# The routing chain between the output projection and the first expert pair: logits turned earlier, one square moved, first gathers by token tile

## What is computed

```
logits = (t @ w_router + b_router)            # 32 experts, t = rmsnorm(x)
top_v, top_i = lax.top_k(logits, TOP_K)       # 4 of 32
wts = softmax(top_v)
z = xb @ w_up[e] + b_up[e]                    # per expert, on its tokens
y = x_glu * sigmoid(1.702 * x_glu) * (x_lin + 1)
out += wts * (y @ w_down[e] + b_down[e])      # then residual and final rmsnorm
```

## Time and profile before

| what | value |
|---|---|
| runs | 1147.6, 1148.07 (median), 1148.33 us |
| span of the profiled execution, first to last instruction | 1146.0 us |
| PE busy | 1113.5 us (97%) |
| DVE, ACT, POOL busy | 311.8, 229.6, 34.0 us |
| HBM read | 436.00 MB |
| mean rate over the span | 383 GB/s |

### The profile page before, as it was taken

One profiled execution on the slowest core, in us unless ns is written; L12 is line 12 of the kernel. 1 busy time (PEld: TensorE's weight loads), 2 busy tenths in 40 slices (PEclk: granted clock), 3 DMA queues, 4 the chain that ended last, 5 costly groups with the idle time before them and its releaser, 6 DMA issues.

```text
span 1146.0 us, 14903 instructions
## 1 busy us (share of the span) xinstructions
PE 1113.5 (97%) x5772; PEld 493.6 (43%) x5772; DVE 311.8 (27%) x785; ACT 229.6 (20%) x642; POOL 34.0 (3%) x69
## 2 busy tenths in 40 slices
PE   8999999999999999999999999999999999999997
PEld 6687778844333424333333333323232323232432
DVE  5665544032131221212130312121213030312123
ACT  4564363422020202010101111111111101010103
POOL 0200012210000000000000000000000000000000
PEclk9999999999999999999999999999999999999999
DMA  9743636989999999999999999999999999999995
GB/s 350 265 153 111 187 112 265 426 350 421 427 428 426 426 427 428 428 428 428 427 428 428 430 429 428 427 428 429 429 429 427 427 428 429 429 427 427 426 427 238
DMA packets 40802, 437.90 MB, mean 382 GB/s; under 512 B 6720, under 2 KB 9040, under 8 KB 11072
## 3 DMA queue, kind: packets, MB, share of 16 engines
q1 hardware_dynamic: 40136, 435.65, 91.2%
q10 hardware_dynamic: 624, 1.68, 0.4%
HBM read 436.00 MB, written 2.41 MB: 383 GB/s over the span
## 4 chain that ended last, share of the span: by engine, by line
PE 69%; DMA 24%; DVE 3%; ACT 2%; issue 1%; DVEq 0%; SPq 0%; ACTq 0%
PE bank L1319 21%; DMA ring<-in_w_down 20%; PE bank L1355 19%; PE bank L1055 8%; PE bank L1100 5%; PE bank L1201 4%; DMA area<-in_w_down 3%; PE bank L1222 3%; PE bank L1150 2%; PE bank L1235 1%; PE bank L1198 1%; PE bank L1036 1%; PE bank L1225 1%; DVE area L1748 1%; PE bank L923 1%
## 5 line engine op out<-in xcount | busy, mean ns | idle before, releaser
L1319 PE MATMUL bank<-ring,area 128*64 128x512 f32 x1744 | 396.4, 597 | 9.1 <-DMA ring<-in_w_up 8.7
L1319 PEld LDWEIGHTS bank<-ring,area 128*64 128x64 f32 x1744 | 117.2, 136 | 261.8 <-issue 222.9
L1355 PE MATMUL bank<-ring,area 128*64 128x512 f32 x928 | 213.7, 599 | 7.5 <-DMA ring<-in_w_down 7.5
L1736 DVE TENSOR_TENSOR x_tok<-x_tok,bank 128x512 f32<-128x512 f32 x60 | 41.3, 688 | 328.0 <-PE bank L1222 328.0
L800 ACT ACTIVATE area<-area 128x256 f32<-128x256 f32 x64 | 26.7, 417 | 516.3 <-DVE area L1748 516.3
L1055 PE MATMUL bank<-ring 128*128 128x264 f32 (+1 forms) x512 | 121.7, 393 | 0.0
L1355 PEld LDWEIGHTS bank<-ring,area 128*64 128x64 f32 x928 | 62.4, 136 | 117.9 <-issue 102.7
L1055 PEld LDWEIGHTS bank<-ring 128*128 128x128 f32 x512 | 95.2, 190 | 21.3 <-issue 4.0
L1773 DVE TENSOR_TENSOR area<-area 128x1024 f32<-128x1024 f32 x15 | 18.4, 1225 | 211.3 <-ACT area L810 211.3
L1222 PE MATMUL bank<-area 128*128 128x512 f32 x128 | 71.8, 644 | 0.0
L1319 PE MATMUL bank<-area 128*64 128x512 f32 x304 | 69.2, 597 | 1.5 <-DMA area<-in_w_up 1.5
(11 more groups left out here) (271 smaller groups left out, 702.6 us busy)
## 6 DMA issues: line engine op xcount, KB each, us to landing
ring<-in_w_up SPq DMA_DIRECT2D x103, 2048.0 KB, 34.3
ring<-in_w_down SPq DMA_DIRECT2D x51, 2048.0 KB, 33.9
area<-in_w_up SPq DMA_DIRECT2D x17, 2048.0 KB, 29.8
ring<-in_w_in SPq DMA_DIRECT2D x16, 1024.0 KB, 9.3
ring<-in_w_down SPq DMA_DIRECT2D x13, 1024.0 KB, 10.6
ring<-in_w_up SPq DMA_DIRECT2D x12, 1024.0 KB, 9.7
area<-in_w_down SPq DMA_DIRECT2D x5, 2048.0 KB, 34.3
ring<-in_w_out SPq DMA_DIRECT2D x8, 1024.0 KB, 5.0
```

What stands on the lines that cost most here:

```text
L1319: m = mm(bank[2 * h + n][64 * e:64 * e + 64, :], xe[:, k, 64 * e:64 * e + 64], w[:, kk, e, NB * n:NB * (n + 1)], start=False, stop=(k == K ...
L1355: m = mm(bank[4 + c][64 * e:64 * e + 64, :], y_t[:, 4 * half + f, 64 * e:64 * e + 64], w[:, f, e, :], start=False, stop=(half == 1 and f = ...
L1736: eng.tensor_tensor(x, x, combined_bank(unit, last)[:, :], ALU.add).then_inc(s.added, 1)
```

## The change

The logits of blocks 0 to 6 are turned by DVE and PE around the eighth block: DVE copies them to `lt` (now in `rs` and `rs_tail`) before it waits for that block, PE multiplies tiles 0 and 1 by `stack` where two dummy matmuls stood, and tile 2 after the transposes. Block 7's logits are computed token-major (`last_logits`) straight into the same PSUM rows. The block's second token tile is turned into bank 4, where DVE copies and squares it; ACT makes the two other squares, copies only tile 0, and takes the first bf16 part from `x_tok`. `rank_m` is made for the first two experts, then the one-hots in three instructions by token tile, then `rank_m` for the other 30. PE has three dummy matmuls instead of four ahead of the gather and waits for `rp_step`, `flag_ready` and `split_copy`; it then goes by token tile, in each tile the slot row, block 0 and block 1 (21 matmuls in all, as before). The dummy matmuls before the biases are four instead of six.

```diff
--- before.py
+++ after.py
@@ -179,7 +179,7 @@
 pt_done pt_evac_a pt_evac_v pv_done pv_evac qd_ready dsc_done dsc_ready dst_done
 q2_ready d_p_ready last_p_tr q2_p_ready d_pv_done d_pv_ready q2_pv_done q2_pv_ready sinkcol_step
 x_biased x_negmax x_sink_exp x_exp x_scaled attn_gated wout_used final_added x2_ready
-split_copy split_sub h2_tr logits_done negtop top_exp selb_ready rank_done flag_ready tables_ready gather_oh weight_oh
+split_copy split_sub h2_tr logits_done negtop top_exp selb_ready rank_done flag_ready tables_ready oh_tile own_rows first_rows rank_ready gather_oh weight_oh
 gather_done xt_ready up_done glu_ready lin_ready sig_ready gated_ready y_ready ytr_done yt_ready gwt_tr
 gwt_ready yd_ready combine_done added ring_used window_stored 
 y_final stored router_step lru_step x_step
@@ -296,10 +296,8 @@
         gw_t, o = at(o, [1, 2 * P + 64])
         assert o == MOE
         y_e, yd, gw_t, rrow = y_e[:, 0, :], yd[:, 0, :], gw_t[:, 0, :], rrow[:, 0, :]
-        lt, o = at(SLOT, [1, 2 * P + 96])
-        lt = lt[:, 0, :]
-        lt_trio = lt[:, 2 * P:2 * P + 96].rearrange("p (i c) -> p i c", i=3)[:, :, 0:B_S]
-        assert o <= 2 * KB * T
+        lt = rs[:, :, :].rearrange("p a b -> p (a b)")
+        lt_trio = rs_tail[:, 0:96].rearrange("p (i c) -> p i c", i=3)[:, :, 0:B_S]
         stack = h0[:, 0:E_N // B_S, :].rearrange("p a b -> p (a b)")
         LG = E_N + TOP_K
         lg, o = at(sig_at, [3, LG])
@@ -756,19 +754,27 @@
             for m in range(KB):
                 tb, cols, half = bank[2 + m % 2], slice(P * m, P * (m + 1)), m // (KB // 2)
                 eng.wait_ge(s.h2_tr, m + 1)
-                for t in range(3):
+                for t in range(3) if m < KB - 1 else (0, 2):
                     n = P if t < 2 else TRIO
                     act(parts[0:n, t % 2, 2 - t // 2, cols], tb[0:n, P * t:P * (t + 1)], ACT.Square, accum_out=ss[0:n, t, m:m + 1])\
                         .then_inc(s.squares, 1)
                 both = tb[:, 0:2 * P].rearrange("p (t c) -> p t c", t=2)
-                act(x_tok[:, :, cols], both, ACT.Copy)
+                if m < KB - 1:
+                    act(x_tok[:, :, cols], both, ACT.Copy)
+                else:
+                    act(x_tok[:, 0, cols], tb[:, 0:P], ACT.Copy).then_inc(s.first_rows, 1)
                 if m == KB - 1:
 
                     eng.wait_ge(s.sumsq, 1)
                     act(stat[:, 6:9], stat[:, 0:3], ACT.Sqrt, bias=eps[:, :], scale=1.0 / D).then_inc(s.root, 1)
-                act(parts[:, :, 0, cols], both, ACT.Copy).then_inc(s.split_copy, 1)
+                if m == KB - 1:
+                    eng.wait_ge(s.own_rows, 1)
+                    eng.wait_ge(s.first_rows, 1)
+                act(parts[:, :, 0, cols], both if m < KB - 1 else x_tok[:, :, cols], ACT.Copy).then_inc(s.split_copy, 1)
                 if m:
                     eng.wait_ge(s.split_copy, 6 * m)
+                if m == KB - 1:
+                    eng.wait_ge(s.logits_done, 3)
                 act(rs_tail[0:TRIO, :], tb[0:TRIO, 2 * P:3 * P], ACT.Copy)
                 act(x_tail[64 * half:64 * half + B_S, P * (m % 4):P * (m % 4 + 1)],
                     tb[64 * half:64 * half + B_S, 2 * P:3 * P], ACT.Copy)
@@ -1116,7 +1122,8 @@
                     eng.wait_ge(s.split_copy, 6 * (m - 2) + 2)
                 tb = bank[2 + m % 2]
                 for t in range(2):
-                    eng.transpose(tb[:, P * t:P * (t + 1)], x_res[:, m, P * t:P * (t + 1)], ident)
+                    dst = tb[:, P * t:P * (t + 1)] if t == 0 or m < KB - 1 else bank[4][:, 0:P]
+                    eng.transpose(dst, x_res[:, m, P * t:P * (t + 1)], ident)
                 eng.wait_ge(s.x2_ready, 3 * m + 2)
                 eng.transpose(tb[0:TRIO, 2 * P:3 * P], xt[:, m % 2, 0:TRIO], ident).then_inc(s.h2_tr, 1)
 
@@ -1130,18 +1137,25 @@
                 eng.wait_ge(s.x2_ready, 3 * m1)
                 for m in range(m0, m1):
                     g = slice(E_N * (m % 4), E_N * (m % 4) + E_N)
-                    ml = mm(raw_lg[g, 0:NT], wr[:, m, :], x_res[:, m, :], start=(m < 4), stop=(m >= 4),
+                    ml = mm(raw_lg[g, 0:NT], wr[:, m, :], x_res[:, m, :], start=(m < 4), stop=(m >= 3),
                             skip_group_check=True)
                 ml.then_inc(s.logits_done, 1)
 
-            def logit_rows():
-
-                eng.wait_ge(s.lt_ready, 1)
+            def logit_rows(t0, t1):
+
+                for t in range(t0, t1):
+                    n = P if t < 2 else TRIO
+                    eng.wait_ge(s.lt_ready, 1 if t < 2 else 2)
+                    own = lt[:, P * t:P * (t + 1)] if t < 2 else rs_tail[:, 0:TRIO]
+                    mm(lg_bank[t][0:n, :], own, stack, start=(t != 1), stop=False, skip_group_check=True)
+
+            def last_logits():
+
+                m = KB - 1
                 for t in range(3):
                     n = P if t < 2 else TRIO
-                    if t == 2:
-                        eng.wait_ge(s.lt_ready, 2)
-                    ml = mm(lg_bank[t][0:n, :], lt[:, P * t:P * t + n], stack, start=True, stop=True)
+                    own = x_res[:, m, P * t:P * (t + 1)] if t < 2 else xt[:, m % 2, 0:TRIO]
+                    ml = mm(lg_bank[t][0:n, :], own, wr[:, m, :], start=False, stop=True, skip_group_check=True)
                 ml.then_inc(s.logits_done, 1)
 
             def biases(n0, n1, b0):
@@ -1152,13 +1166,13 @@
 
             for m in range(KB):
                 out_block(m)
-            keep_warm(2, bank[0])
+            logit_rows(0, 2)
             token_rows(KB - 1)
-            logits(KB - 1, KB)
-            logit_rows()
-
-
-            keep_warm(6, bank[0])
+            logit_rows(2, 3)
+            last_logits()
+
+
+            keep_warm(4, bank[0])
             eng.wait_ge(s.tables_ready, 3)
             eng.wait_ge(s.bias_step, 5)
             eng.wait_ge(s.split_copy, 6 * (KB - 1) + 2)
@@ -1287,20 +1301,35 @@
 
             def first_rows(j):
 
-                if j == 1:
+                eng.wait_ge(s.xt_ready, j - 1)
+                gather(0, (j,), 6 + j % 2).then_inc(s.gather_done, 1)
+
+            def pair(q, full, pipelined, first=False, last=False, gamma=False):
+
+                if first:
+
+                    keep_warm(3, bank[5])
+                    eng.wait_ge(s.rp_step, 9)
                     eng.wait_ge(s.flag_ready, 1)
-                if j >= 2:
-                    eng.wait_ge(s.xt_ready, j - 1)
-                gather(0, (j,), 6 + j % 2).then_inc(s.gather_done, 1)
-
-            def pair(q, full, pipelined, first=False, last=False, gamma=False):
-
-                if first:
-
-                    keep_warm(4, bank[5])
-                    slot_rows(q, 5)
-                    first_rows(0)
-                    first_rows(1)
+                    eng.wait_ge(s.split_copy, 12)
+                    for t in range(3):
+                        if t < 2:
+                            eng.wait_ge(s.oh_tile, t + 1)
+                        else:
+                            eng.wait_ge(s.gather_oh, 1)
+                        own, k = ((rp[:, :, t], P) if t < 2 else (rt[0:TRIO, 0:1], TRIO))
+                        for i in range(3 if t < 2 else 1):
+                            m = mm(bank[5][:, 0:P], own[:, i:i + 1].to_broadcast([k, P]), g_oh[0:k, t, :],
+                                   start=(t == 0 and i == 0), stop=(t == 2))
+                        if t == 2:
+                            m.then_inc(s.rrow_done, 1)
+                        for j in range(2):
+                            for i in range(3 if t < 2 else 1):
+                                left = parts[:, t, i, P * j:P * (j + 1)] if t < 2 else h_tail[0:TRIO, P * j:P * (j + 1)]
+                                m = mm(bank[6 + j][:, P * j:P * (j + 1)], left, g_oh[0:k, t, :],
+                                       start=(t == 0 and i == 0), stop=(t == 2))
+                            if t == 2:
+                                m.then_inc(s.gather_done, 1)
                 else:
                     eng.wait_ge(s.y_ready, 4 * q)
                     eng.wait_ge(s.xe_ready, 2 * q)
@@ -1658,7 +1687,15 @@
 
             eng.wait_ge(s.x_loaded, 16)
             eng.wait_ge(s.zeroed, 10)
+            router_step = stepper(s.router_step)
             for m in range(KB):
+                if m == KB - 1:
+                    eng.wait_ge(s.split_copy, 6 * m)
+                    router_step(eng.memset(rs_tail[:, 0:96], 0.0))
+                    eng.wait_ge(s.logits_done, 2)
+                    eng.tensor_copy(lt, raw_lg[:, 0:2 * P]).then_inc(s.lt_ready, 1)
+                    eng.tensor_copy(lt_trio, raw_lg[:, 2 * P:NT].unsqueeze(1).to_broadcast([P, 3, B_S]))\
+                       .then_inc(s.lt_ready, 1)
                 eng.wait_ge(s.wout_used, m + 1)
                 out = bank[m % 2]
                 if m >= 2:
@@ -1672,20 +1709,20 @@
```

(44 more changed lines are left out.)

## The result

| | median | lowest to highest | runs |
|---|---|---|---|
| kernel before | 1147.84 us | 1146.85 to 1148.33 | 4 |
| changed kernel | 1158.88 us | 1158.52 to 1159.03 | 4 |

The ratio is 1.0098 (95% interval 1.0085 to 1.011): slower by 11 us, where +0.7 was forecast. Of all executions on record one stands far off, 3984.56 us, of the kernel before on the chip of the first four experiments, and it is in none of the ratios. The span of the profiled execution is 1157.2 us. The part that the prediction worked through is 0.6 us longer; the rest of the 11 us comes from a place that it didn't look at.

The account below looks back on a forecast made before the run. The prediction took the DMA weight stream, stalled until PE's first expert matmul, as the bound. Gather +0.16 (after -0.46 and -0.09) and slot row +0.52 gave +0.68: 1148.07 became 1148.75, said as 1148.7, range 1147.3 to 1150.0 us.

Parts of the forecast that it names:

- that one moment: PE's first expert matmul, at 237.44 us before; SP's next load follows it, so its +0.68 us shift would reach the end.
- All five cases: Whole-kernel outcomes: chain 0.3 to 1.0 longer 0.74, hidden anyway 0.10, shorter chain 0.06, lower clock 0.05, block 7's add late 0.05.
- the one on the clock: Pair 0's start: PE idle with three dummies drops TensorE's clock to 1.2 GHz, giving 1152.4 us; chance 0.05.
- The logits turned early: Around block 7: DVE's copies of blocks 0 to 6 end at 228.3, hidden by 0.8 us of cover before its add.
- Scaling 0.46 earlier: Scaling of the logits after block 7: starts at 231.70 instead of 232.16, -0.46 us, bounds -0.60 and -0.30.
- The 0.13 that I allowed: DVE's moved square: 0.13 us extra for its accumulator read-out, with the reduce at 230.95 instead of 231.14.
- The small `rank_m`: Ranks ahead of the one-hots: for two experts, next start 0.20 us later instead of 0.29, -0.09.
- The one-hots: DVE's one-hots in three instructions beside POOL: 0.97 us instead of 0.80, +0.17; without the POOL share 0.71.
- The gather 0.16 later: PE's first gather matmul: waits for the flag DVE sets last, starts at 236.03 instead of 235.87.
- The slot row behind nineteen matmuls: PE's gather: slot row complete after 19 matmuls instead of 7, 0.67 later, less 0.15 of DVE waiting, +0.52 us.
- One to one: Routing chain to the end: changes up to 237.44 us pass on fully until 2 us of idle are used; losses always.
- The order of the two bounds: Expert pairs: PE lives off the stock of loads first and is paced by the DMA weight stream later.

Follow-up runs that it names:

- the first four experiments: Changed kernel with three more PE instructions or its loop at slot 0; kernel before with four fewer or its loop at slot 128: 1148.18, 1148.31, 1156.74, 1153.32 us.
- experiment 11: Changed kernel, PE's loop at slot 0, slot rows first, other 30 ranks after the scalings, POOL's block 7 parts after the one-hots: 1146.63 us, ratio 0.9994.
- experiment 1: Changed kernel with three more PE instructions at the start, so its loop begins at the same number as in the kernel before: 1148.18 us, ratio 1.0004.
- experiment 3: Changed kernel with PE's loop placed at the first slot of a 256-instruction block: 1148.31 us, ratio 1.0006.
- slot 128: Kernel before with PE's loop placed at slot 128 of a 256-instruction block: 1153.32 us, ratio 1.0048.
- slot 32: Changed kernel with PE's loop placed at slot 32 of a 256-instruction block: 1151.15 us, one execution.
- experiment 2: Kernel before with 12 instead of 14 dummy matmuls at its start, four PE instructions fewer: 1156.74 us, ratio 1.0084.

## Why the prediction was wrong

**The step that failed** is the first one: "The change is judged by that one moment." It took for granted that the sixteen pairs behind it run as before, because no line of them was edited. All five cases, with the whole of the chance, take the loop as it was, and the one on the clock looks only at the start of pair 0; the range ended at 1150.0. The runs showed a cost in its place that depends on the number of PE instructions ahead of the loop. Dummies, turned logits and waits together made it three fewer, the body then reached into an eighth block and each of three jumps back cost 8.4 to 8.8 us of standing still and up to 2.6 of a lowered clock. Nothing in the trace of before warned of it, but its page shows instruction fetches, and 28 packets against a loop of four rounds meant that the body was held and not fetched again. I had not asked how near to the limit.

**The chain** came out by its steps. Its sum was +0.68; it measured +0.57 (8.90 against 8.33).
- The logits turned early were hidden, DVE's copies ended 0.83 us before block 7, the forecast cover was 0.8.
- Scaling 0.46 earlier: it was 0.57, near the bound of -0.60. DVE's accumulator read-out exists, as an instruction of its own. The Trainium skill, "VectorE: DVE Perf Modes", section "Two Vector instructions with no wait between them", counts such an instruction as two, and the trace agrees. But its 0.08 us end where the square's own 0.29 end, so it costs nothing. The 0.13 that I allowed for it were too much, and the reduce starts 0.31 earlier in the chain and not 0.19.
- The small `rank_m`: next start 0.20 later, as said. The one-hots: 0.93 against 0.97. The cost beside POOL was real, 0.23 by experiment 11, where the three took 0.70 (my sum without POOL was 0.71).
- The gather 0.16 later: 0.06 later, the 0.11 better of the scaling. It followed the flag and not a tile.
- The slot row behind nineteen matmuls: its copy came 0.66 later after the gather's start; 0.67 was forecast, less the 0.15 of waiting that went.

**One to one.** SP's next load moved with the first expert matmul (1.97 us behind it in both). With the stops out of the way, the changed kernel is 0.60 us (experiment 1) and 0.73 (experiment 3) above the kernel before, for 0.57 in the chain. Both intervals hold 1, so that it reaches the end agrees and is not shown.

**The clock.** At the start of pair 0 it was 1.00, so the rival in its own form was wrong. A clock of 0.50 came all the same, behind stops that only the loop has.

**The order of the two bounds.** PE's waits for weights were slack of 20.6 us; without it three stops would have cost 32.5. That PE is paced by the stream was right, and it is why a loss of 32.5 on PE shows as 11. But slack does not hide a stop whole: with slot 128 three stops of together 8.4 us, well under 20.6, cost 5.7 us although PE still waits for weights (7.4 us on the line shown), and with slot 32 one of 4.0 us cost 3.5 (one execution). Why is open.

## What to carry to other kernels

Before and after any edit ahead of a large loop, compare the fetched instruction packets on the page: more of them with the same loop means that the jump back misses. Count the body and its place, or pin the loop's head so that the body lies in as few blocks as it can; 1767 instructions fit seven blocks only with the head in slots 0 to 25, and here an edit of three instructions fell out of that. And a wait placed ahead of a pipelined sequence decides for all of it: ask which of its results is set last.

## What the runs showed of the hardware

- A jump back that misses stops PE for 2.7 to 3.0 us (4.0 once, with slot 32) with the head in the middle of its block and, with it within four instructions of the block's end, for 7.7 to 9.1 us, at 425 GB/s of other traffic. Where the long stop is split, its first part is 2.6 to 2.9 us of idle matmul time (experiment 2) and its second 5.3 to 5.9 between two weight loads (experiment 2 and the changed kernel).
- PE idle for 8.4 us but for one weight load brought the clock to 0.50, and the first matmuls of the next pair ran at it. After stops of 2.7 and 3.0 us it stayed at 1.00, after another of 2.7 us it fell to 0.64 for a window of 4 us.
- The same DVE one-hots took 0.93 us beside POOL's two-input subtractions and 0.70 without them.
- The chain from block 7's add to the first expert matmul repeats to 0.02 us from one execution to another (8.33 in three traces, 8.89 to 8.90 in six), far finer than the time of the whole, so that one trace settles an edit of a tenth.
